# Selection masks built in one block behind the search, the l2 norm ahead of the tile copies, and an earlier first mixer load

## The chip, the core and the metric

The kernel runs on one core of a Trainium2 chip. Its engines work from queues of their own, in program order: PE (TensorE, matrix products into PSUM), ACT (ScalarE), DVE (VectorE), POOL (GpSimd), and SP (SyncE), which only issues DMAs here. They wait for each other by semaphores. The metric is device time of the program, in microseconds, as the median of the runs.

## The reference

Two layers of a streaming encoder run on 1,024 prompt tokens and on 8 x 16 sample tokens that carry caches and states, 1,152 tokens in all, 1,024 channels wide. A layer normalizes and modulates the tokens and makes one combined input projection. From it come three kinds of heads: gated DeltaNet (a delta rule in chunks of 64), softmax attention over selected keys, and an SSD mixer (Mamba-2, chunks of 64). Their outputs are joined by one output projection; a gated convolutional FFN follows.

What the change touches:

```
q, k = l2_normalize(silu(conv(q))), l2_normalize(silu(conv(k)))        # DeltaNet
score = sum_h relu(qi_h . ki) * wi_h          # indexer, per query and key
_, sel = top_k(score, 256)                    # ties go to the earlier key
att = softmax over the selected keys only
```

The kernel doesn't gather. For each block of 128 queries it finds the 256th largest score by a bitwise search, and builds a mask that is 0 at selected keys and -1e30 at all others; attention adds it to the logits.

## The kernel before

Channels lie on the partitions, tokens along the free dimension. One queue is written out by hand for each engine; all order below is program order.

**The dense tiles.** The input projection of a layer is 27 tiles of 128 output channels by 1,152 tokens, in `project` (L804), each from eight blocks of weights, into two PSUM sets in turn. Tile n+2 needs ACT's copy of tile n out of its set (`proj_evac`). Tiles 0 to 6 are rotated keys and queries; 7 and 22 to 26 are gates (`silu_tile`); 8 to 21 go through a causal convolution: ACT's `conv_rows` copies the tile into one of two `ext` buffers and makes the last tap, DVE's `conv` adds the other three, ACT's `conv_silu` finishes it.

**The l2 norm.** Five pieces i = 0 to 4 of q and k are squared by ACT (`l2_square`, in tile 9 + i), summed over each head by PE behind tile 10 + i (`l2_sums`, L927, into the same two PSUM banks each time), turned into 1/sqrt by ACT in tile 11 + i (`l2_scale`: Ln at L1550, Exp at L1552) and multiplied in by DVE (`l2_scaled`). `l2_sums(i)` waits for `l2_scale(i - 1)` (`l2_rs`). Piece 4 has 512 columns, the others 1,024.

**The search.** Seven score blocks (six of prompt queries with 384 to 1,024 keys, one of sample queries with 1,040; 5,264 columns together) are searched for the threshold `T`, 31 bits from the top. In a round DVE's `offer` makes a candidate and counts the first four blocks (L1880); ACT's `count_far` (L1560) counts the other three; DVE's `decide` waits for it and keeps or drops the bit. `ROUNDS` says how many rounds go with each tile from 8 on; DVE runs what is left after tile 21 without a break, ACT ahead of its gate tiles. `search_ties` ends the search. In tiles 16 to 18 PE also makes decay rows (`DEC_AT`), which DVE and ACT turn into decays; in 19 to 21 it makes key products (`KK_AT`), whose second pair waits for DVE's result of the first.

**After the tiles.** DVE zeroes `rt` (L2021, in the space of hT, so it waits for the last tile), multiplies the attention products by the decays (PE's L945 makes the products), then scales PE's natural copies of k (L982). POOL meanwhile inverts 32 x 32 blocks by elimination (L2371, L2373). SP loads the inverse into `rt` (L661) once it is zeroed. PE joins the blocks (L1003, L1009, then L1016), and the 16 DeltaNet chunks run.

**The masks.** `mask_piece(k, j)` is one of four pieces of the mask of block j: `mask_count` (a comparison with a count, L2048, a small instruction and an equality, L2051), `mask_scan` (running sum of equal scores, L2056), `mask_ties` and `mask_write` (L2068 last), seven instructions in all beside drains. Blocks 0 and 1 are done before the DeltaNet chunks; the pieces of blocks 2 to 6 are dealt out between the steps of the SSD mixer by `search()`: one behind the first state update of a tile and two behind its outputs. `t_cum` and `t_eq`, their working space, lie in hT.

**The SSD mixer.** Nine tiles of 128 tokens. For each PE makes decay rows and transposes (`ssd_rows`), ACT copies and exponentiates (`ssd_decay`), POOL scales (`ssd_scaled`, L2409, L2410) and carries the state (L2423), DVE adds the states, prepares (`ssd_prep`) and makes the outputs, ACT norms them (`ssd_norm`). SP's `load_s(t)` brings tile t into one of three slots `sl`, in turn; the first three are loaded once the DeltaNet output is done (`g_out`). The attention follows; PE waits for `mask_ready` ahead of its first logits.

Of the kernel before, what the change touches and what calls it, by code (L numbers as in the profile page):

```python
# [13 lines left out]
TOK = TPR + NB * TS  # L14
# [5 lines left out]
TOPK = 256  # L20
# [9 lines left out]
BIG = 1.0e30  # L30
# [2 lines left out]
NU, NUP = 36, 32  # L33
GW = 24
G_G, G_DT, G_BETA = 0, 12, 20
ROUNDS = {8: 2, 9: 2, 10: 2, 11: 2, 12: 2, 13: 2, 14: 2, 15: 2, 16: 1, 17: 1, 18: 1, 19: 1, 20: 1, 21: 1, 22: 3, 23: 3, 24: 3}
FAR = (4, 5, 6)
SHARED = sum(ROUNDS.values())
DEC_AT = {16: (0, 1), 17: (2, 3), 18: (4, 5)}
# [120 lines left out]
def build(nc, a):  # L160
# [3 lines left out]
    with ctx:  # L164
# [59 lines left out]
        one_t = sb("one_t", [128, 1])  # L224
# [195 lines left out]
        def turned(d, i):  # L420
            return ptb[d % 2][:, 512 * i:512 * i + 512]

        t_cum = hw[:, 0:1040]
        t_eq = hw[:, 1040:2080]
        far_signs = {j: xw[:, o:o + SC_N[j] // 2].bitcast(bf16) for j, o in ((4, 7952), (5, 7432), (6, 7432))}


# [39 lines left out]

            return ap.rearrange("p h (c t) -> p h c t", t=64)

        sl = [z.rearrange("p (c k x) -> p c k x", c=2, k=12) for z in (xw[:, 7432:8968], hw[:, 4840:6376], big[:, 2 * TOK:2 * TOK + 1536])]  # L470

        def two_tiles(x, c, k):

# [13 lines left out]
        hs_scaled = [big[:, o_qk + 1024 * q:o_qk + 1024 * q + 1024] for q in range(3)] + [fext[:, 0:1024]]  # L487
        def tile_in(t):

            return sl[(t + 1) % 3], sl_in[(t + 1) % 3], t // 3 + 1  # L490

        hb = [xw[:, 4096 + 512 * i:4608 + 512 * i] for i in range(3)]
        h_end = xw[:, 5632:6144]
# [64 lines left out]
        def _(sp):  # L558
# [28 lines left out]
            for l in range(NL):  # L587
# [92 lines left out]
                sp.wait_ge(*g_wtc.at(l, 5))  # L680
                for hp in range(2):
                    sp.dma_start(gt[:, hp, :], a["scr"][14 + hp]).then_inc(*gt_in.up())
                sp.wait_ge(*g_out.at(l, 3))
                for t in range(3):
                    load_s(t)
                sp.dma_start(hs, a["sstate"][l]).then_inc(*state_in.up())
                for t in range(3, NT):
# [703 lines left out]
        def _(sc):  # L1391
# [61 lines left out]
            for l in range(NL):  # L1453
# [91 lines left out]
                def l2_scale(i):  # L1545
                    m = TPR if i < 4 else 512
                    sc.wait_ge(*l2_sum.at(l, i + 1))
                    if i:
                        sc.wait_ge(*l2_mul.at(l, i))
                    act_(l2r[:, 0:m], PS[:, 3072:3072 + m], ACT.Ln, bias=eps_t[:, :])  # L1550
                    dr()
                    act_(l2r[:, 0:m], l2r[:, 0:m], ACT.Exp, scale=-0.5).then_inc(*l2_rs.up())  # L1552
# [10 lines left out]

                silu_tile(NROT)
                for n in range(LEAD, LEAD + NCONV):
                    conv_rows(n)
                    if 0 <= n - LEAD - 3 < 5:
                        l2_scale(n - LEAD - 3)
                    if n > LEAD:
                        conv_silu(n - 1)  # L1570
                        if n - LEAD - 1 < 5:
                            l2_square(n - LEAD - 1)
                    for k in DEC_AT.get(n, ()):
                        sc.wait_ge(*g_diff.at(l, k + 1))
                        x = dec_piece(k)
                        act_(x, x, ACT.Exp).then_inc(*g_dec.up())
                    for i in range(ROUNDS[n]):
                        count_far()
# [173 lines left out]
        def _(dv):  # L1752
# [57 lines left out]
            for l in range(NL):  # L1810
# [201 lines left out]
                for bit in bits:  # L2012
                    offer(bit)
                    decide(bit)
                search_ties()
                if l == 0:
                    dv.wait_ge(ada_kept.sem, 7)
                    add_bias(16, 28, mod)
# [22 lines left out]
                    dv.wait_ge(*g_eg.at(l, 3 * hp + 3))  # L2041
                    tt_(qkv[:, hp, :], qkv[:, hp, :], eg_row[:, hp, :], ALU.mult)
                dr().then_inc(*g_qe.up())
                def mask_count(j):
                    n = SC_N[j]
                    sco = scores[:, SC_OFF[j]:SC_OFF[j] + n]
                    thr = T[:, j:j + 1].bitcast(f32)
                    V.tensor_scalar(t_eq[:, 0:n], sco, thr, 0.0, ALU.is_gt, ALU.add, accum_out=CNT[:, j:j + 1])  # L2048
                    dr()
                    V.tensor_scalar(NEED[:, j:j + 1], CNT[:, j:j + 1], -1.0, float(TOPK), ALU.mult, ALU.add)  # L2050
                    V.tensor_scalar(t_eq[:, 0:n], sco, thr, None, ALU.is_equal)  # L2051
                    dr()

                def mask_scan(j):
                    n = SC_N[j]
                    V.tensor_tensor_scan(t_cum[:, 0:n], one_t[:, 0:1].to_broadcast([128, n]), t_eq[:, 0:n], 0.0, ALU.mult, ALU.add)  # L2056
                    dr()

                def mask_ties(j):
                    n = SC_N[j]  # L2060
                    stt(t_sel[:, 0:n], t_cum[:, 0:n], NEED[:, j:j + 1], t_eq[:, 0:n], ALU.is_le, ALU.mult)
                    dr()

                def mask_write(j):
                    n = SC_N[j]
                    stt(t_eq[:, 0:n], scores[:, SC_OFF[j]:SC_OFF[j] + n], T[:, j:j + 1].bitcast(f32), t_sel[:, 0:n], ALU.is_gt, ALU.add)
                    dr()
                    V.tensor_scalar(masks[:, SC_OFF[j]:SC_OFF[j] + n], t_eq[:, 0:n], -1.0, BIG, ALU.add, ALU.mult)  # L2068
                    dr()

                def mask_piece(k, j):
                    if k == 0:
                        mask_count(j)
                    elif k == 1:
                        mask_scan(j)
                    elif k == 2:
                        mask_ties(j)
                    else:
                        mask_write(j)

                for j in range(2):
                    for k in range(4):
                        mask_piece(k, j)

                V.memset(gS, 0.0)
                dr().then_inc(*g_s.up())
# [40 lines left out]
                    stt(mixT[:, 0:2, c0:c0 + m], o_n[:, :, c0:c0 + m], par[:, P_GNG:P_GNG + 1], gt[:, :, c0:c0 + m], ALU.mult, ALU.mult)  # L2127
                    dr().then_inc(*g_out.up())

                searched = []  # L2130

                def search():

                    k = len(searched)
                    j = 2 + k // 4
                    if j < 7:
                        searched.append(k)
                        mask_piece(k % 4, j)

                def ssd_prep(t):  # L2140

                    dv.wait_ge(*s["acted"].at(l, t + 1))
# [7 lines left out]
                for t in range(NT):  # L2150
                    if t < 8:
                        dv.wait_ge(*s["st"].at(l, t + 1))
                        for c in range(2):
                            n = 2 * t + c
                            dv.wait_ge(*s["he"].at(l, n + 1))
                            tt_(by_group(hb[(n + 1) % 3]), by_group(h_end), PS[:, 3072:4096].rearrange("p (g c x) -> p g c x", g=2, c=2)[:, :, c, :],
                                ALU.add).then_inc(*s["h"].up())
                            if c == 0:
                                search()
                        ssd_prep(t + 1)  # L2160
                    dv.wait_ge(*s["y"].at(l, t + 1))
                    need(dv, *s["nrm"].at(l, t))
                    tt_(eight(y1), eight(bank(5)), b3(gs[:, EGC, t, :], 64), ALU.mult)
                    dr()
                    tt_(y1, y1, bank(4), ALU.add)
                    dr()
                    tt_(y1, y1, bank(3), ALU.mult)
                    dr().then_inc(*s["y2"].up())
                    search()
                    search()  # L2170
                dv.wait_ge(*s["he"].at(l, 17))
                for q in range(4):
                    dv.wait_ge(*s["hs"].at(l, q + 1))
# [2 lines left out]
                        PS[:, 3072:4096].rearrange("p (g b x) -> p b g x", g=2, b=2)  # L2176
                    tt_(two, hs_scaled[q].rearrange("p (b g x) -> p b g x", b=2, g=2), new, ALU.add).then_inc(*s["hsd"].up())

                while len(searched) < 4 * 5:
                    search()  # L2180
                dr().then_inc(*mask_ready.up())


                V.memset(qz, 0.0)
                dr()
                for h in range(4):
# [414 lines left out]
```

## Time and profile before

| | us |
|---|---|
| median of three runs | 4369.09 (4368.46 to 4374.56) |
| the profiled execution, its time | 4367.9 |
| its span in the profile | 4365.8 |
| mean granted clock of TensorE in it | 0.961 |

The span is what the profiler saw between the first and the last instruction; the execution's own time has 2.1 us around it. Times in the rows below are microseconds from the start of the span. The first layer's dense tiles 7 to 26 run from about 296 to 667, its SSD mixer from about 755 to 880; the second layer repeats this some 2,150 us later.

### The profile page before, as it was taken

The numbers are of one execution on the slowest core, as the hardware profiler recorded it, in microseconds if no ns is written. First come the engines' busy times: TensorE is split into PE (matmuls) and PEld (weight loads), VectorE is DVE, ScalarE is ACT, GpSimd is POOL, SyncE is SP. The second block draws the span as 40 slices with busy tenths as digits, with TensorE's granted clock in tenths as the row PEclk, the third lists the DMA queues.
The fourth block names the chain that finished last, engine by engine and source line by source line (L and its number), as shares of the span: only waits on it lengthen the run. The fifth ranks groups of instructions, "written<-read, shape, count | busy, mean of one in ns | idle before, by whom it ended". The sixth has DMA issues, their size and how long they took to land.

```text
span 4365.8 us, 49384 instructions
## 1 busy us (share of the span) xinstructions
PE 4051.1 (93%) x20340; PEld 2189.5 (50%) x20340; DVE 1397.9 (32%) x2792; ACT 979.6 (22%) x1659; POOL 260.9 (6%) x384
## 2 busy tenths in 40 slices
PE   6788898889999999999999979978899999999998
PEld 3454456645455555555545435565454555554554
DVE  2236674662311111100022456647513212121001
ACT  2026662431100000000011366434301000000000
POOL 0000031400000000000000000414000000000000
PEclk9899998899999999999999989978999999999999
DMA  5410133142122122111122101423311111111111
GB/s 200 114 60 29 36 96 99 59 175 102 60 97 87 59 68 68 59 51 42 57 74 76 59 25 56 123 74 113 117 41 41 34 34 34 34 34 32 36 36 52
DMA packets 186849, 299.48 MB, mean 69 GB/s; under 512 B 89056, under 2 KB 140448, under 8 KB 180224
## 3 DMA queue, kind: packets, MB, share of 16 engines
q1 hardware_dynamic: 182144, 279.35, 19.5%
q0 software_dynamic: 3904, 12.27, 0.9%
q10 hardware_dynamic: 576, 4.72, 0.3%
q8 instruction: 160, 2.62, 0.3%
q14 instruction: 65, 0.53, 0.0%
HBM read 245.30 MB, written 42.47 MB: 66 GB/s over the span
## 4 chain that ended last, share of the span: by engine, by line
PE 87%; DVE 4%; ACT 2%; issue 2%; POOL 1%; DMA 1%; DVEq 1%; ACTq 1%; SPq 1%; POOLq 0%
PE PS L804 51%; PE PS L1380 16%; PE PS L1351 6%; PE PS L832 2%; PE PS L782 1%; PE PS L1227 1%; DVE big L1768 1%; PE PS L927 1%; DVE xT L1771 1%; PE PS L1281 1%; PE PS L1305 1%; POOL xT L2423 1%; DVE hT L1771 1%; PE PS L1264 1%; PE PS L1246 1%
## 5 line engine op out<-in xcount | busy, mean ns | idle before, releaser
L804 PE MATMUL PS<-hT,ring 128*128 128x512 f32 (+1 forms) x6816 | 2243.7, 491 | 34.6 <-ACT hT L1449 21.2
L804 PEld LDWEIGHTS PS<-hT,ring 128*128 128x128 f32 x6816 | 1135.3, 192 | 1152.1 <-issue 1138.0
L1380 PE MATMUL PS<-big,ring 128*128 128x512 f32 (+1 forms) x2112 | 683.5, 487 | 2.5 <-DVE big L1771 2.5
L1380 PEld LDWEIGHTS PS<-big,ring 128*128 128x128 f32 x2112 | 346.6, 191 | 339.4 <-issue 336.5
L1768 DVE SCALAR_TENSOR_TENSOR xT<-PS,mod,xT 128x1024 f32<-128x1024 f32 x32 | 41.1, 1284 | 856.9 <-PE PS L1380 642.0
L1437 ACT ACTIVATE hT<-xT 128x1152 f32<-128x1152 f32 x40 | 46.3, 1162 | 929.0 <-DVEq L2288 804.2
L1351 PE MATMUL PS<-big,ring 128*128 128x512 f32 (+1 forms) x768 | 250.3, 487 | 1.0 <-DVEq L2227 1.0
L2316 DVE TENSOR_SCALAR big<-fext,par 128x1024 f32<-128x1024 f32 x44 | 35.7, 812 | 671.2 <-ACTq L1736 671.2
L1560 ACT ACTIVATE xT<-big,tk 128x1024 bf16<-128x1024 f32 x186 | 223.5, 1202 | 52.0 <-DVEq L1908 47.2
L1734 ACT ACTIVATE fext<-PS 128x1024 f32<-128x1024 f32 x44 | 45.1, 1025 | 839.8 <-PE PS L804 839.8
L1880 DVE TENSOR_SCALAR_CACHE_REDUCE xT<-big,tk 128x384 bf16<-128x384 f32 (+6 forms) x268 | 222.8, 832 | 28.0 <-issue 0.9
L1771 DVE TENSOR_TENSOR big<-big,PS 128x1152 f32<-128x1152 f32 x44 | 59.6, 1354 | 442.0 <-PE PS L804 442.0
L1351 PEld LDWEIGHTS PS<-big,ring 128*128 128x128 f32 x768 | 126.7, 191 | 124.7 <-issue 123.2
L2454 POOL DMA_DIRECT2D out_o_ftail<-ftail x44 | 23.8, 540 | 1918.3 <-DVEq L2326 1918.3
L1768 DVE SCALAR_TENSOR_TENSOR big<-fext,par,big 128x1024 f32<-128x1024 f32 (+1 forms) x176 | 136.1, 815 | 6.8
L1740 ACT ACTIVATE big<-big 128x1152 f32<-128x1152 f32 x44 | 51.2, 1163 | 193.6 <-DVEq L2322 193.6
L927 PE MATMUL PS<-big,cf 128*128 128x512 f32 x36 | 30.4, 986 | 60.1 <-ACT big L1552 60.1
L782 PE MATMUL PS<-ring,silc 128*32 128x128 f32 x1536 | 63.4, 301 | 23.9 <-DMA ring<-in_w_ada 22.7
L1768 DVE SCALAR_TENSOR_TENSOR big<-big,par 128x1024 f32<-128x1024 f32 x96 | 74.3, 816 | 33.7 <-ACTq L1529 30.7
L1771 DVE TENSOR_TENSOR xT<-xT,PS 128x512 f32<-128x512 f32 (+2 forms) x108 | 58.7, 548 | 65.1 <-PE PS L1177 23.9
L1768 DVE SCALAR_TENSOR_TENSOR xT<-big,par,xT 128x1024 f32<-128x1024 f32 x72 | 55.7, 814 | 65.5 <-ACTq L1529 63.4
L832 PE MATMUL PS<-big,hT 128*128 128x276 f32 x288 | 67.8, 395 | 0.3 <-ACT mod L1417 0.3
(384 smaller groups left out, 3253.4 us busy)
## 6 DMA issues: line engine op xcount, KB each, us to landing
ring<-in_w_ada SPq DMA_DIRECT2D x96, 512.0 KB, 4.9
ring<-in_w_in SPq DMA_DIRECT2D x54, 512.0 KB, 5.2
ring<-in_w_gate SPq DMA_DIRECT2D x44, 512.0 KB, 3.5
ring<-in_w_up SPq DMA_DIRECT2D x44, 512.0 KB, 3.5
ring<-in_w_down SPq DMA_DIRECT2D x32, 448.0 KB, 3.3
d_x<-big SPq DMA_DIRECT2D x24, 576.0 KB, 4.6
ring<-in_kidx SPq DMA_DIRECT2D x16, 512.0 KB, 4.8
ring<-in_w_out SPq DMA_DIRECT2D x16, 512.0 KB, 5.6
```

The source lines that it names most:

```text
L782: i = mm(PS[32 * m:32 * m + 32, where:where + 128], silc[:, 2 * q + k, :], w[:, m, k, :], start=(q == 0 and k == 0), stop=(q == 3 and k == 1))
L804: i = mm(pset(n % 2)[:, c0:c0 + m], w[:, k, :], hT[:, k, c0:c0 + m], start=(k == 0), stop=(k == KT - 1))
L832: i = mm(bank(7 - t % 2, VW), hT[:, k, t * 128:(t + 1) * 128], wv[:, k, :], start=(k == 0), stop=(k == KT - 1))
L927: x = mm(PS[:, 3072 + c0:3584 + c0], b64, l2s[i % 2][:, c0:c0 + 512], start=True, stop=True)
L1351: i = mm(pset(m % 2)[:, c0:c0 + n], w[:, k, :], mixT[:, k, c0:c0 + n], start=(k == 0), stop=(k == KT - 1))
L1380: i = mm(pset(m % 2)[:, c0:c0 + n], w[:, k - k0, :], act[:, k * TOK + c0:k * TOK + c0 + n], start=(k == 0), stop=(k == NF - 1))
L1437: act_(sqb[k % 2], xT[:, k, :], ACT.Square).then_inc(*sq_ready.up())
L1560: act_(far_signs[j], scores[:, SC_OFF[j]:SC_OFF[j] + SC_N[j]], ACT.Sign, scale=SCALE[:, j:j + 1], bias=BIAS[:, j:j + 1], accum_out=CNT[:, ...
L1740: act_(aj, aj, ACT.Silu).then_inc(*ff_silu.up())
L1768: return V.scalar_tensor_tensor(out=out, in0=in0, scalar=scalar, in1=in1, op0=op0, op1=op1)
L1771: return V.tensor_tensor(out, in0, in1, op)
L1880: V.tensor_scalar(t_sel[:, 0:SC_N[j]], scores[:, SC_OFF[j]:SC_OFF[j] + SC_N[j]], limit[:, j:j + 1].bitcast(f32), 0.0, op, ALU.add, accum_o ...
```

## The change

All seven masks are built in one block on DVE right behind `search_ties`, and `mask_ready` is signalled there; the pieces are gone from before the DeltaNet chunks and from the SSD steps, with `search()` itself. Since hT is still read by the last dense tiles at that point, `t_cum` and `t_eq` move to the two `ext` buffers. `ROUNDS` gives tiles 16, 18 and 20 a second round, and tile 24 loses its three: six rounds in place of nine are left after tile 21. On ACT, `l2_scale` comes ahead of `conv_rows` in the same tile. On SP, `load_s(0)` goes ahead of the wait for `g_out`, and the slots change places so that tile 0 lies in free space.

```diff
-ROUNDS = {8: 2, 9: 2, 10: 2, 11: 2, 12: 2, 13: 2, 14: 2, 15: 2, 16: 1, 17: 1, 18: 1, 19: 1, 20: 1, 21: 1, 22: 3, 23: 3, 24: 3}
+ROUNDS = {8: 2, 9: 2, 10: 2, 11: 2, 12: 2, 13: 2, 14: 2, 15: 2, 16: 2, 17: 1, 18: 2, 19: 1, 20: 2, 21: 1, 22: 3, 23: 3}
...
-        t_cum = hw[:, 0:1040]
-        t_eq = hw[:, 1040:2080]
+        t_cum, t_eq = [ext[p][:, 0:1040] for p in range(2)]
...
-        sl = [z.rearrange("p (c k x) -> p c k x", c=2, k=12) for z in (xw[:, 7432:8968], hw[:, 4840:6376], big[:, 2 * TOK:2 * TOK + 1536])]
+        sl = [z.rearrange("p (c k x) -> p c k x", c=2, k=12) for z in (xw[:, 7432:8968], big[:, 2 * TOK:2 * TOK + 1536], hw[:, 4840:6376])]
...
-            return sl[(t + 1) % 3], sl_in[(t + 1) % 3], t // 3 + 1
+            return sl[t % 3], sl_in[t % 3], t // 3 + 1
...
                     sp.dma_start(gt[:, hp, :], a["scr"][14 + hp]).then_inc(*gt_in.up())
+                load_s(0)
                 sp.wait_ge(*g_out.at(l, 3))
-                for t in range(3):
+                for t in range(1, 3):
                     load_s(t)
...
                 for n in range(LEAD, LEAD + NCONV):
-                    conv_rows(n)
                     if 0 <= n - LEAD - 3 < 5:
                         l2_scale(n - LEAD - 3)
+                    conv_rows(n)
                     if n > LEAD:
...
                 search_ties()
+
+                def mask_count(j):
...
+                for j in range(7):
+                    mask_count(j)
+                    mask_scan(j)
+                    mask_ties(j)
+                    mask_write(j)
+                dr().then_inc(*mask_ready.up())
                 if l == 0:
                     dv.wait_ge(ada_kept.sem, 7)
                     add_bias(16, 28, mod)
...
-                for j in range(2):
-                    for k in range(4):
-                        mask_piece(k, j)
...
                                 ALU.add).then_inc(*s["h"].up())
-                            if c == 0:
-                                search()
...
                     dr().then_inc(*s["y2"].up())
-                    search()
-                    search()
...
-                while len(searched) < 4 * 5:
-                    search()
-                dr().then_inc(*mask_ready.up())
+                dr()
```

The four functions `mask_count` to `mask_write` are moved unchanged.

## Rows read from the trace of the kernel before

**Rows 1.** The page: span, and costliest groups (busy us, mean ns, idle before, releaser).
```profile
span 4365.8 us, 49384 instructions
...
L927 PE MATMUL PS<-big,cf 128*128 128x512 f32 x36 | 30.4, 986 | 60.1 <-ACT big L1552 60.1
```
**Rows 2.** Windows around PE's head sums: length, busy time per engine, granted clock.
```profile
360.80:362.80 2.00, 2.00 (x8) 1.04 (x7) 1.77 (x5) 1.70 (x3) 0.00 (x0) 1.00 0.36 92
...
385.77:389.52 3.75, 3.75 (x5) 1.68 (x6) 1.44 (x3) 3.65 (x4) 0.00 (x0) 0.50 0.00 0
```
**Rows 3.** Timeline of ACT, tiles 11 and 12: start, length, instruction, [idle before <-releaser].
```profile
374.32 0.19 ACT L1560 ACTIVATION_READ_ACCUMULATOR xT<-big,tk 128x1 f32 x1
...
380.81 1.28 ACT L1550 ACT_TABLE_LOAD   x1
...
385.64 1.28 ACT L1533 ACT_TABLE_LOAD   x1
...
405.41 1.02 ACT L1523 ACTIVATE big<-PS 128x1024 f32<-128x1024 f32 x1 [7.15 <-PE PS L804]
...
424.85 0.18 ACT L1560 ACTIVATION_READ_ACCUMULATOR xT<-big,tk 128x1 f32 x1
```
**Rows 4.** Timeline of DVE, tile 15 to the zeroing of rt.
```profile
500.12 3.43 DVE L1771 TENSOR_TENSOR tk<-tk 128x7 f32<-128x7 f32 x1
...
524.00 0.17 DVE L1771 TENSOR_TENSOR tk<-tk 128x7 int32<-128x7 f32 x1 [4.48 <-ACTq L1562]
...
555.31 0.17 DVE L1771 TENSOR_TENSOR tk<-tk 128x7 int32<-128x7 f32 x1 [4.48 <-ACTq L1562]
...
591.27 4.79 DVE L1768 SCALAR_TENSOR_TENSOR big<-big,par 128x1024 f32<-128x1024 f32 x6 [3.73 <-ACTq L1529]
...
597.65 0.17 DVE L1771 TENSOR_TENSOR tk<-tk 128x7 int32<-128x7 f32 x1
...
602.55 0.17 DVE L1771 TENSOR_TENSOR tk<-tk 128x7 int32<-128x7 f32 x1 [0.30 <-ACTq L1562]
...
645.36 0.21 DVE L1771 TENSOR_TENSOR tk<-tk 128x7 int32<-128x7 f32 x1 [0.30 <-ACTq L1562]
...
667.75 1.98 DVE L2021 MEMSET hT<- 128x2304 f32 x1 [15.55 <-PE PS L804]
```
**Rows 5.** Timeline of DVE, the masks of blocks 0 and 1.
```profile
688.58 0.61 DVE L2048 TENSOR_SCALAR_CACHE_REDUCE hT<-big,tk 128x384 f32<-128x384 f32 x1
...
692.73 0.75 DVE L2048 TENSOR_SCALAR_CACHE_REDUCE hT<-big,tk 128x512 f32<-128x512 f32 x1
...
693.63 0.48 DVE L2051 TENSOR_SCALAR hT<-big,tk 128x512 f32<-128x512 f32 x1
...
704.30 0.29 DVE L1771 TENSOR_TENSOR big<-PS,gq 128x128 f32<-128x128 f32 x1 [6.44 <-PE PS L1042]
```
**Rows 6.** Timeline of PE: attention products, first join, first SSD tile.
```profile
668.44 4.42 PE L945 MATMUL PS<-xT 64*64 64x64 f32 x144 [1.24 <-ACTq L1514]
...
687.19 2.21 PE L1003 MATMUL PS<-xT,hT 32*32 32x32 f32 x128 [0.69 <-ACT hT L1597]
...
759.49 0.48 PE L1118 MATMUL PS<-hT 128*64 128x64 f32 x4 [0.78 <-DMA hT<-d_x]
```
**Rows 7.** Timeline of SP: the first loads into rt.
```profile
673.71 2.69 SPq L661 DMA_DIRECT2D hT<-d_r  x4
```
**Rows 8.** Windows of the SSD steps: all eight tiles, two single steps.
```profile
778.07:872.99 94.92, 80.92 (x988) 57.18 (x988) 65.54 (x81) 45.19 (x166) 46.71 (x43) 0.84 0.17 54
...
789.36:801.90 12.54, 12.54 (x123) 8.76 (x123) 8.43 (x13) 4.82 (x18) 5.07 (x5) 0.59 0.03 11
...
852.13:862.48 10.35, 8.73 (x126) 6.14 (x125) 6.04 (x9) 6.46 (x24) 5.98 (x7) 1.00 0.01 2
```
**Rows 9.** Timelines in layer 0: a DVE mask instruction beside POOL; a POOL elimination.
```profile
824.11 2.32 DVE L2051 TENSOR_SCALAR hT<-big,tk 128x1024 f32<-128x1024 f32 x1
...
633.23 0.70 POOL L2373 TENSOR_TENSOR big<-big,xT 128x255 f32<-128x255 f32 x1
```

More of the change, by code:

```diff
@@ L2015, in _, with mask_scan, mask_ties, mask_write @@
                 search_ties()
+                def mask_count(j):
+                    n = SC_N[j]
+                    sco = scores[:, SC_OFF[j]:SC_OFF[j] + n]
+                    thr = T[:, j:j + 1].bitcast(f32)
+                    V.tensor_scalar(t_eq[:, 0:n], sco, thr, 0.0, ALU.is_gt, ALU.add, accum_out=CNT[:, j:j + 1])
+                    dr()
+                    V.tensor_scalar(NEED[:, j:j + 1], CNT[:, j:j + 1], -1.0, float(TOPK), ALU.mult, ALU.add)
+                    V.tensor_scalar(t_eq[:, 0:n], sco, thr, None, ALU.is_equal)
+                    dr()
+                def mask_scan(j):
+                    n = SC_N[j]
+                    V.tensor_tensor_scan(t_cum[:, 0:n], one_t[:, 0:1].to_broadcast([128, n]), t_eq[:, 0:n], 0.0, ALU.mult, ALU.add)
+                    dr()
+                def mask_ties(j):
+                    n = SC_N[j]
+                    stt(t_sel[:, 0:n], t_cum[:, 0:n], NEED[:, j:j + 1], t_eq[:, 0:n], ALU.is_le, ALU.mult)
+                    dr()
+                def mask_write(j):
+                    n = SC_N[j]
+                    stt(t_eq[:, 0:n], scores[:, SC_OFF[j]:SC_OFF[j] + n], T[:, j:j + 1].bitcast(f32), t_sel[:, 0:n], ALU.is_gt, ALU.add)
+                    dr()
+                    V.tensor_scalar(masks[:, SC_OFF[j]:SC_OFF[j] + n], t_eq[:, 0:n], -1.0, BIG, ALU.add, ALU.mult)
+                    dr()
+                for j in range(7):
[4 more added lines that the diff above has]
+                dr().then_inc(*mask_ready.up())
                 if l == 0:
@@ L2043, in _ @@
                 dr().then_inc(*g_qe.up())
[L2044 to L2079, printed above, removed]
-                for j in range(2):
-                    for k in range(4):
-                        mask_piece(k, j)
                 V.memset(gS, 0.0)
@@ L2128, in _ @@
                     dr().then_inc(*g_out.up())
[L2130 to L2138, printed above, removed]
                 def ssd_prep(t):
@@ L2177, in _ @@
                     tt_(two, hs_scaled[q].rearrange("p (b g x) -> p b g x", b=2, g=2), new, ALU.add).then_inc(*s["hsd"].up())
-                while len(searched) < 4 * 5:
-                    search()
-                dr().then_inc(*mask_ready.up())
+                dr()
                 V.memset(qz, 0.0)
```

## The prediction

> **What bounds the kernel now.** The page first: PE is busy nearly all the span, but its line for the head sums (L927, `l2_sums`) is small in work and large in idle time before it: 60.1 us behind ACT's L1552, the last instruction of `l2_scale` [rows 1]. The code says where: four sums in each of two layers, so 7.5 us apiece, after dense tiles 11 to 14. In the windows the reader sees what the wait does to PE: the first set of sums runs in 2.0 us at a granted clock of 1.00 (2.4 GHz), the next, behind 7.5 us of idling, in 3.75 us at 0.50 (1.2 GHz) [rows 2].
>
> ACT's timeline explains the wait [rows 3]. ACT counts for the search until 374.5, then idles until tile 11 is out of PE; it copies that tile, and only then (380.81) begins the two table loads, Ln and Exp of the norm, done at 385.64. PE stands through copy and norm. At tile 12 ACT idled 7.15 us before the copy, time in which the 4.83 us norm would have fitted.
>
> DVE's timeline gives the search [rows 4]: one decision every 15.65 us in tiles 16 to 18, then nine rounds of 5.3 us on average, an end at 652.2 and 15.55 us of idling until PE has left hT. Then come the masks of blocks 0 and 1 [rows 5], the joins [rows 6], and the SSD steps, where the other five masks are cut into pieces [rows 8].
>
> **The norm ahead of the copies.** Nothing is added; PE no longer waits for copy plus norm. ACT then becomes the limit: its whole chain for a tile, from the copy at 405.41 to the end of the second count at 425.03, is 19.6 us with norm, copies, Silu, square and both counts [rows 3], in any order. Today some 7.5 us of idling come on top, 27.1 a tile; of these PE works 15.9 on the tile itself (27.1 less 7.5 of wait and 3.75 of sums [rows 2]) and, kept busy, 2.0 on the sums. So a tile takes 19.6 us in place of 27.1, with PE idling under 2 us in each. What is queued behind the norm on ACT is the copy of the tile just made; the norm's own input has been there since the tile before, so it doesn't hold the copy. PE's gain is some 30 us a layer at tile 15. It is worth that only if the search and everything behind it on ACT and DVE keeps up, so I follow this chain to the point where PE needs DVE again.
>
> **Search and masks.** From 374.5: tiles 11 to 14 at 19.6 give 452.9; tile 15 (half the norm, no square) about 17.5: 470.4. There DVE was held 3.4 us in a seven-element instruction [rows 4], right where the code lets POOL begin its decay products (L2387, after `l2_mul`); the same can be expected: 473.8. Tiles 16 to 18 at 15.65, and a second round in 16 and in 18 at 4.9 each (the step from 597.65 to 602.55): 530.6. Tiles 19 to 21 took 42.3 together (555.31 to 597.65), of which 3.7 was a wait for PE that is gone when DVE is late, and 20 gets a second round: 574.1. In the trace this is 597.65: DVE's chain keeps 23.5 of the 30 us. Six rounds are left in place of nine, at 5.3 (nine took 47.7): 605.9. From the last decision to the search's end is 6.8: 612.7.
>
> Mask 0 takes 4.15 us for 384 columns; mask 1 and a zeroing of 0.2 end 6.44 us before 704.30, which leaves it 4.95 for 512 [rows 5]: 0.8 more for each 128. Over the 5,264 columns of all seven that makes 45.2 us. The ext buffers that now hold sums and equalities change no instruction's size. POOL eliminates blocks under the first four masks (its elimination starts when tile 21's products are done, and shifts with them); in a mask made beside POOL one comparison of 1,024 columns took 2.32 us, where 512 columns took 0.48 alone, and POOL's own instructions are at most 0.70 there [rows 5, 9]. Below, contention costs nothing; above, five of a mask's seven instructions each wait out one such instruction, 14 us over four masks. I take 3, because the search's small instructions beside POOL lengthened a round from 4.9 to only 5.3 on average. So the masks end at 661.
>
> PE would be through its tiles near 640 (30 us off, less some 3 for which tile 20's products wait for the later DVE). It finds DVE in the masks: behind them are queued the zeroing of rt, the attention products (on which PE's natural copies wait) and thereby SP's block loads. So PE stands some 20 us: most of what the norm freed is given back here. What counts is the zeroing: 661 in place of 667.75.
>
> From the zeroing to the first join, PE's L1003, it is 19.4 us now [rows 4, 6]. PE has the 4.4 us of L945 [rows 6] behind it by then, as well as part of the natural copies: at best 15.0. But it has idled, and rows 2 show half clock after 7.5 us of that: at worst 20, all as slow as it gets back. I take 17.3. SP's first block load went out at 673.71 [rows 7], and all had landed by 687.19, within 13.5 us; now the first can go at about 663, so they are in by 676.5. The join is then at 678.3 in place of 687.2: 8.9 us a layer.
>
> **Masks gone from the mixer steps.** Blocks 0 and 1 begin at 688.58, under PE's joins, which start at 687.19, and behind them DVE waits 6.44 us for PE [rows 5, 6]: removing them gives nothing there. In the SSD steps eight tiles take 94.9 us [rows 8]. The two windows show the kinds of step: 10.35 us at clock 1.00, where the loop is the y products, ACT's norm and decay, POOL's scaling, DVE's state; and 12.54 us at 0.59, where PE is busy throughout. Without pieces of masks, DVE is never late. All steps of the first kind: 82.8, a gain of 12.1; alternating kinds: 91.6, a gain of 3.3. In the first kind PE idles only 1.6 us, so I take 8.
>
> **The early mixer load.** One issue on SP moves ahead of a wait; SP's later loads are not delayed by it, and the other two slots change places at equal sizes. PE's wait for this load is 0.78 us [rows 6]: 0.8 gained, because PE first makes its decay rows, which hid the rest of the transfer. Masks ready earlier serve nobody: PE and SP ask for them after the SSD outputs. The moved bias addition (0.3 us in layer 0) is read much later.
>
> **Sum.** 8.9 + 0.8 + 8 = 17.7 us a layer; the second layer shows the same wait, so 35.4. The profiled execution took 4367.9 (span 4365.8), 1.2 below the median of 4369.09, a difference smaller than what counts here: 4332. About 0.2% (9 us) is what a measurement of this kernel tells from no change.
>
> Bounds: masks from 654.8 (no POOL hold, no contention) with a join 15.0 later and SSD 12.1 give 30.3 a layer, 4307. Masks at 675.8 (all 14 us, and a second hold of 3.4) with 20 and 3.3 lose 4.5 a layer, 4377.
>
> **Rivals.** *Masks held by POOL:* contention is the full 14 us, the masks end at 672, the join at 689.3, 2.1 us later than now; 8.8 stays from the other two, 6.7 a layer: 4354. For it speaks the 2.32 us comparison; against it the search's rounds. 0.18.
> The Trainium skill, SBUF — State Buffer, section Who interferes with whom, says that a VectorE instruction with two SBUF inputs, or in a two-port mode, shuts out a GpSimd instruction that reads SBUF, and the reverse, for its whole length. By that rule the five contending instructions of each mask would wait, and this rival's time would hold; the 2.32 us row agrees with a whole-length block, while the mean lengthening of a round doesn't tell.
>
> *More comes through:* no hold, no contention, PE quick after its wait, SSD all at the short step: 4307 as in the bound. Against it: the hold is in the trace, and the code's order keeps it. 0.17.
>
> *No change:* the time is only moved to the zeroing of rt. That takes masks ending 17.7 us later, near 679: 4368. Seven masks would have to take 66 us. 0.07.
>
> *Slower:* ACT's queue doesn't let the norm go early, since the second count waits for DVE's candidate, and the norm still ends 7.5 us behind PE's tile. Tiles 11 to 14 then keep 27.1 us, the masks end at 691, the join at 708.3, 21.1 us late: 12.3 lost a layer, 4392. It decides when each of these tiles saves under 3.1 of 7.5 us. Against it stand 7.15 us of idle ACT before the copy. 0.06.
>
> **How the numbers follow.** The forecast has 0.52, with a range of its own of 4320 to 4347 (masks 3 us either way, SSD 4). Outward to hold 8 in 10: 4308 takes in nearly the better case, 4356 the held masks. Faster: 0.52 + 0.18 + 0.17 = 0.87; same 0.07; slower 0.06.
>
> **What would show it.** L927 without idle time of more than 2 us and its sums under 2.1 us; the first tile copies 19 to 20 us apart in tiles 11 to 14; the search's end near 613 and the zeroing of rt near 661, straight behind the last mask, with no wait for PE; PE idle for 15 to 20 us behind tile 26; L1003 near 678; SSD steps of 10 to 11.5 us; no wait for the first SSD load. The prediction is wrong if DVE still idles before the zeroing, if the masks take over 55 us, or if the tile spacing stays above 22.

## The result, and the profile after

The change makes the kernel 0.9% faster: 4331.0 us, median of five runs (4326.9 to 4341.48), against 4369.09 for the kernel before; the ratio is 0.9915, with a 95% interval from 0.9899 to 0.9931. Forecast were 4332, in a range of 4308 to 4356. The profiled execution took 4328.62 us.

First two lines of the kernel before: the chain that ended last by engine, from its page, and the line of the head sums (least, median and greatest duration in ns, first and last start):

```profile
PE 87%; DVE 4%; ACT 2%; issue 2%; POOL 1%; DMA 1%; DVEq 1%; ACTq 1%; SPq 1%; POOLq 0%
```

```profile
L927 PE MATMUL PS<-big,cf x36: 592/1061/1193, 360.9 to 2618.8; 128*128 128x512 f32 x36
```

The same of the kernel after, with its span, and with PE's idle time before the head sums and the number of waits:

```profile
span 4326.8 us, 49376 instructions
...
PE 75%; DVE 10%; ACT 6%; issue 3%; DVEq 1%; ACTq 1%; POOL 1%; DMA 1%; SPq 0%; POOLq 0%
```

```profile
L927 PE MATMUL PS<-big,cf x36: 592/593/1061, 367.4 to 2574.3; 128*128 128x512 f32 x36
its engine sat idle before it (us, times) until:
  ACT big L1552: 11.1, 8
```

The 60.1 us in front of the head sums [rows 1] are down to 11.1, and the median of these products is down from 1061 ns to 593. But the chain that ends last now runs less over PE and more over the others: PE's share is down from 87% to 75%, DVE's is up from 4% to 10% and ACT's from 2% to 6%. In this execution all of the first layer runs some 6.5 us later than in the one before: the first head sums begin at 367.4 in place of 360.9, ahead of which the code is the same. Times of the first layer below stand as the trace gives them; the prediction's have 6.5 to be added.

ACT's timeline of the kernel after shows the norm's first table load (L1550) ahead of the copy of tile 11 (L1523), and the copies of tiles 12 to 14, each 19.9, 19.6 and 19.0 us behind the one before it. Its last three lines are the norm's first load in tile 15, the second count of tile 15 and the copy of tile 16:

```profile
381.06 1.28 ACT L1550 ACT_TABLE_LOAD   x1
...
385.78 1.01 ACT L1523 ACTIVATE big<-PS 128x1024 f32<-128x1024 f32 x1
...
405.72 1.00 ACT L1523 ACTIVATE big<-PS 128x1024 f32<-128x1024 f32 x1
...
425.31 1.01 ACT L1523 ACTIVATE big<-PS 128x1024 f32<-128x1024 f32 x1
...
444.27 1.00 ACT L1523 ACTIVATE big<-PS 128x1024 f32<-128x1024 f32 x1
...
458.33 1.28 ACT L1550 ACT_TABLE_LOAD   x1
...
475.22 1.24 ACT L1560 ACTIVATE xT<-big,tk 128x1024 bf16<-128x1024 f32 x1 [4.34 <-DVEq L1908]
...
479.25 1.02 ACT L1523 ACTIVATE big<-PS 128x1024 f32<-128x1024 f32 x1 [0.16 <-issue]
```

DVE's timeline of the kernel after: the instruction held in tile 15, the decision of tile 21 and the last decision of the search, the first mask instruction, a scan beside POOL, the zeroing of rt, and the first instruction of the DeltaNet chunks.

```profile
471.43 3.48 DVE L1905 TENSOR_SCALAR tk<-tk 128x7 int32<-128x7 int32 x1
...
580.33 0.17 DVE L1771 TENSOR_TENSOR tk<-tk 128x7 int32<-128x7 f32 x1
...
611.26 0.17 DVE L1771 TENSOR_TENSOR tk<-tk 128x7 int32<-128x7 f32 x1 [0.30 <-ACTq L1562]
...
618.72 0.61 DVE L2021 TENSOR_SCALAR_CACHE_REDUCE big<-big,tk 128x384 f32<-128x384 f32 x1
...
644.69 3.64 DVE L2029 TENSOR_TENSOR_SCAN big<-one_t,big 128x896 f32<-128x896 f32 x1
...
669.32 1.98 DVE L2055 MEMSET hT<- 128x2304 f32 x1 [0.59 <-issue]
...
702.86 0.29 DVE L1771 TENSOR_TENSOR big<-PS,gq 128x128 f32<-128x128 f32 x1 [16.05 <-PE PS L1042]
```

Where DVE idled 15.55 us for PE [rows 4], it now goes from the search into the masks and from these into the zeroing. The one that waits is PE, as its timeline behind tile 26 shows:

```profile
648.25 4.42 PE L945 MATMUL PS<-xT 64*64 64x64 f32 x144 [1.24 <-ACTq L1514]
652.50 2.97 PE L982 MATMUL PS<-cf,xT 64*64 64x64 f32 x96
672.13 7.57 PE L982 MATMUL PS<-cf,xT 64*64 64x64 f32 x192 [16.67 <-DVE hT L1771]
...
685.22 2.21 PE L1003 MATMUL PS<-xT,hT 32*32 32x32 f32 x128 [0.69 <-ACT hT L1597]
```

PE is through its tiles 20 us sooner than before on the clock (648.25 against 668.44 [rows 6]), stands 16.67 us, and joins only 2.0 sooner (8.4 with the later start taken off). The windows of the SSD steps (length; busy time and count of PE, weight loads, DVE, ACT and POOL; granted clock, DMA share, GB/s), the same stretch as in [rows 8] and a single step:

```profile
775.12:858.38 83.26, 70.03 (x988) 50.33 (x988) 30.35 (x46) 45.19 (x166) 39.98 (x43) 0.98 0.18 62
785.48:795.84 10.36, 8.83 (x128) 6.25 (x127) 4.04 (x6) 5.96 (x22) 4.13 (x5) 1.00 0.23 77
```

Eight steps take 83.3 us in place of 94.9, all of them of the short kind.

To compare the kernels, distances between first instructions free the stages from the start. "Join" is from the first head sum (L927) to the first join (L1003); "SSD" is from the first products of the SSD mixer (L1118) to the first outputs of its last tile (L1192). First and second layer are given apart; the differences are to the kernel before on the same chip (median). The kernels in the lower rows are those of the experiments.

| kernel | us | to the kernel before | join | SSD |
|---|---|---|---|---|
| before | 4369.09 | | 326.3 / 327.3 | 109.8 / 109.7 |
| after | 4331.0 | -38.1 | 317.9 / 314.9 | 97.1 / 98.6 |
| norm alone | 4305.73 | -67.1 | 295.5 / 294.6 | 109.8 / 105.0 |
| norm late | 4402.34 | +29.5 | 351.9 / 351.0 | 97.0 / 96.8 |
| spread | 4315.82 | -57.0 | 298.3 / 297.4 | 109.4 / 109.5 |
| spread, outputs | 4291.98 | -80.9 | 296.8 / 299.6 | 97.0 / 97.0 |
| spread, gaps | 4290.37 | -82.5 | 296.0 / 294.2 | 96.9 / 98.9 |
| no elimination | 4317.75 | -55.1 | 311.3 / 309.6 | 99.1 / 98.6 |

From the first head sums to the output projection (first L1351) the layers went from 656.5 and 658.6 us to 635.7 and 634.4: 20.8 and 24.2 gained.

### The profile page after: what moved, and what is told of

Same layout as the page of the kernel before. It is cut to its first block, busy times and chain, and to the rows that moved or that the text cites. A ratio compares the mean times of both kernels' runs of the same rounds, so it can differ in the third digit from the quotient of the medians.

```text
span 4326.8 us, 49376 instructions
## 1 busy us (share of the span) xinstructions
PE 4025.7 (93%) x20330; PEld 2178.6 (50%) x20340; DVE 1394.8 (32%) x2792; ACT 978.3 (23%) x1659; POOL 279.3 (6%) x384
## 3 DMA queue, kind: packets, MB, share of 16 engines
q1 hardware_dynamic: 182144, 279.35, 19.6%
## 4 chain that ended last, share of the span: by engine, by line
PE 75%; DVE 10%; ACT 6%; issue 3%; DVEq 1%; ACTq 1%; POOL 1%; DMA 1%; SPq 0%; POOLq 0%
PE PS L804 40%; PE PS L1380 16%; PE PS L1351 6%; ACT xT L1560 3%; DVE big L1768 2%; PE PS L832 2%; DVE xT L1880 1%; PE PS L782 1%; PE PS L1227 1%; DVE big L1771 1%; POOL xT L2401 1%; PE PS L1281 1%; PE PS L1305 1%; DVE xT L1771 1%; DVE big L2029 1%
## 5 line engine op out<-in xcount | busy, mean ns | idle before, releaser
L1351 PE MATMUL PS<-big,ring 128*128 128x512 f32 (+1 forms) x768 | 250.3, 487 | 1.0 <-DVEq L2205 1.0
L1351 PEld LDWEIGHTS PS<-big,ring 128*128 128x128 f32 x768 | 126.7, 191 | 124.7 <-issue 123.2
L782 PE MATMUL PS<-ring,silc 128*32 128x128 f32 x1536 | 62.5, 298 | 24.7 <-DMA ring<-in_w_ada 24.2
L1469 ACT ACTIVATE big<-PS 128x1152 f32<-128x1152 f32 x14 | 15.8, 1130 | 216.5 <-PE PS L804 115.5
```

What stands on the lines that cost most here:

```text
L782: i = mm(PS[32 * m:32 * m + 32, where:where + 128], silc[:, 2 * q + k, :], w[:, m, k, :], start=(q == 0 and k == 0), stop=(q == 3 and k == 1))
L1351: i = mm(pset(m % 2)[:, c0:c0 + n], w[:, k, :], mixT[:, k, c0:c0 + n], start=(k == 0), stop=(k == KT - 1))
```

## The experiments

**The norm alone, and everything but the norm.** The first kernel is the one before with only the norm moved; the second is the change with the norm back behind the copies.

```diff
 # norm alone (on the kernel before); norm late is the reverse (on the kernel after)
                 for n in range(LEAD, LEAD + NCONV):
-                    conv_rows(n)
                     if 0 <= n - LEAD - 3 < 5:
                         l2_scale(n - LEAD - 3)
+                    conv_rows(n)
```

> The kernel before with the norm ahead of the tile copies and nothing else. My theory, that the later of PE's tiles and DVE's chain sets the zeroing of rt: the search ends within 5 us of where it does with the whole change (as many rounds, in another order), some 25 us before PE is through its tiles; DVE waits there for PE, the zeroing of rt comes near 645, and the join 19.4 behind it. That is 27 to 30 us a layer, with the SSD steps as before: 4309 to 4315. Rival, that the norm in itself brings only what the whole change gained up to the join (8.5 and 12.5 us in the two layers): 4348. Rival, that only the idle time in front of the head sums comes back (49 us in all): 4320.

> The whole change, but the norm behind the copies as before: the masks' block, the rounds and the early load without the norm. My theory: tiles 11 to 14 take 27.1 us again, the search ends near 648 to 655, the masks take 49.6 behind it, PE stands some 30 us behind tile 26, and the join comes 25 to 30 us later than before; the SSD gives 13 back and the attention loses 1.4. Some 15 us a layer are lost: 4390 to 4408. Rival, that the block is hidden by DVE's 15.6 us of idling and by PE's tiles: only the SSD gain shows, 4345.

Measured: 4305.73 for the norm alone, ratio 0.9849 (0.9834 to 0.9864), and 4402.34 for the rest without it, ratio 1.0059 (1.0043 to 1.0076). DVE and PE of the norm alone:

```profile
642.71 1.98 DVE L2021 MEMSET hT<- 128x2304 f32 x1 [15.35 <-PE PS L804]
```

```profile
643.41 4.42 PE L945 MATMUL PS<-xT 64*64 64x64 f32 x144 [1.24 <-ACTq L1514]
...
662.99 2.21 PE L1003 MATMUL PS<-xT,hT 32*32 32x32 f32 x128 [0.70 <-ACT hT L1597]
```

One moved call on ACT is worth more than the whole change: the join comes 31 and 33 us sooner. DVE waits for PE, and PE no longer for DVE. The theory holds, and its two rivals fall. The gain, 67.1 us, is above the 54 to 60 expected, since the join came sooner than the 27 to 30 us a layer that I had; in the second layer the SSD mixer is also 4.8 us shorter than in the first with the same code, and why stays open. One part of the theory was wrong: the search ended at 627.1, 8.3 us later behind the first head sums than with the whole change, where I had said within 5; that leads to the last experiment. PE of the norm late:

```profile
710.83 7.46 PE L982 MATMUL PS<-cf,xT 64*64 64x64 f32 x192 [17.03 <-DVE hT L1771]
```

The masks' block then ends at 707 and the join comes 25.6 and 23.7 us later than before, while the SSD gains its 12.8 all the same. The time is as expected, but PE's wait is 17.03 us and not some 30. The block behind the search is a loss that the norm pays for.

**The masks where DVE idles.** Blocks 0 to 3 stay behind the search, block 4 goes ahead of the DeltaNet chunks, 5 and 6 into the SSD steps in pieces, one a step behind the first state update. This version and the two that follow keep the early load and deal the rounds out as the kernel before does; behind the block the working space is back in hT, and `mask_ready` is signalled behind the SSD mixer. The cuts below leave these lines out.

```diff
-                for j in range(7):
+                for j in range(4):
                     mask_count(j)
...
+                for piece in pieces:
+                    piece(4)
                 V.memset(gS, 0.0)
...
                             dv.wait_ge(*s["he"].at(l, n + 1))
                             tt_(...).then_inc(*s["h"].up())
+                            if c == 0:
+                                pieces[t % 4](5 + t // 4)
```

> The norm early and the masks spread over the places where DVE idles: blocks 0 to 3 behind the search, block 4 ahead of the DeltaNet chunks (16.05 us of idling there), the pieces of blocks 5 and 6 one per SSD step behind its first state update (3.6 us of idling there); rounds as before, the early load kept. My theory: the block behind the search ends near 643, PE's tiles near 645, so PE no longer stands there; the join comes 17 us a layer earlier than with the whole change, and the SSD steps stay near 10.4 us: 4289 (4283 to 4300). Rival, that POOL's elimination or SP's loads hold the join near 680 anyway: 4320 or more. Rival, that pieces in the SSD steps cost there what they cost before: 4312.

Measured: 4315.82, ratio 0.9868 (0.9853 to 0.9883), near the last rival. The join came as expected; the SSD didn't gain anything (109.4), with one piece a step in place of three. POOL's timeline of a step shows why, with DVE's mask instructions of that step in the second fence. The third fence is a step of the next kernel, in which the pieces stand elsewhere (lines are one lower in these two kernels):

```profile
784.71 1.95 POOL L2391 TENSOR_TENSOR hT<-hT,gaf 128x512 f32<-128x512 f32 x1 [5.25 <-ACT hT L1634]
786.63 1.49 POOL L2392 TENSOR_TENSOR hT<-hT,gaf 128x512 f32<-128x512 f32 x1
788.29 1.04 POOL L2405 TENSOR_TENSOR xT<-xT,gaf 128x512 f32<-128x512 f32 x1 [0.18 <-issue]
```

```profile
784.48 1.28 DVE L1767 SCALAR_TENSOR_TENSOR hT<-big,tk,xT 128x1024 f32<-128x1024 f32 x1
785.84 1.37 DVE L2040 TENSOR_SCALAR big<-hT 128x1024 bf16<-128x1024 f32 x1
```

```profile
778.50 1.04 POOL L2391 TENSOR_TENSOR hT<-hT,gaf 128x512 f32<-128x512 f32 x1 [5.24 <-ACT hT L1634]
779.51 1.04 POOL L2392 TENSOR_TENSOR hT<-hT,gaf 128x512 f32<-128x512 f32 x1
780.73 1.04 POOL L2405 TENSOR_TENSOR xT<-xT,gaf 128x512 f32<-128x512 f32 x1 [0.18 <-issue]
```

DVE idles behind the first state update, but it does so because POOL scales there, and the step waits for POOL's L2405. The two instructions of a mask piece beside POOL's stretch two of these by 0.91 and 0.45 us, 1.4 us of this step; the eight steps together take 12.4 us more than with the pieces elsewhere.

**The same pieces behind the outputs, and no pieces between the steps.**

```diff
 # spread, outputs
-                            if c == 0:
-                                pieces[t % 4](5 + t // 4)
...
                     dr().then_inc(*s["y2"].up())
+                    if t < 8:
+                        pieces[t % 4](5 + t // 4)
 # spread, gaps: blocks 0 to 2 behind the search, 3 and 4 ahead of the chunks, and
+                for piece in pieces:
+                    piece(5)
                 ssd_prep(0)
...
                         ssd_prep(t + 1)
+                    else:
+                        for piece in pieces:
+                            piece(6)
```

> The spread masks once more, with one thing moved: the pieces of blocks 5 and 6 go from behind the first state update of an SSD step to behind the outputs of the tile, where DVE idles 2.35 us and POOL idles too. Theory 1, that a piece costs there nothing, and that behind the state update it cost by stretching POOL's scaling (1.04 to 1.95 us): the eight SSD steps come from 109.4 (first L1117 to first L1191) to 97 to 100, the join stays; 18 to 24 us less in all than with the pieces behind the state update, 75 to 81 under the kernel before. Rival, that any piece in a step costs its own length: no change, 57 under the kernel before.

> No pieces in the SSD steps at all: blocks 0 to 2 behind the search, 3 and 4 ahead of the DeltaNet chunks, 5 ahead of the first SSD preparation (8.5 us of idling), 6 in the last SSD tile ahead of its outputs (8.5 us of idling). Theory 1: PE waits for none of them; SSD 97 to 99, join 295 to 297 behind the first head sums; 78 to 84 under the kernel before, the best of all. Rival, that these gaps are too short with POOL at work beside them: 1 to 3 us lost at each of the three places, 65 to 75 under the kernel before.

Measured: 4291.98, ratio 0.9821 (0.9806 to 0.9836), and 4290.37, ratio 0.9817 (0.9803 to 0.9832). Both times lie where they were expected. The first version moves one thing and the SSD falls from 109.4 and 109.5 to 97.0 in both layers, about what it takes without any piece: the place of a piece was the whole cost, not its length. DVE's timeline of that kernel shows the last piece of a mask, two instructions, between the outputs and the state update; DVE is through 0.19 us before PE releases it:

```profile
785.61 1.28 DVE L1767 SCALAR_TENSOR_TENSOR hT<-big,tk,xT 128x1024 f32<-128x1024 f32 x1
786.97 0.69 DVE L2040 TENSOR_SCALAR big<-hT 128x1024 bf16<-128x1024 f32 x1
787.85 0.69 DVE L1770 TENSOR_TENSOR xT<-xT,PS 128x512 f32<-128x512 f32 x1 [0.19 <-PE PS L1176]
```

In the second, DVE has made three masks and zeroes rt all the same within 0.4 us of PE's first attention products (its own timeline, then PE's):

```profile
642.97 1.98 DVE L2056 MEMSET hT<- 128x2304 f32 x1 [0.59 <-issue]
```

```profile
642.64 4.41 PE L944 MATMUL PS<-xT 64*64 64x64 f32 x144 [1.24 <-ACTq L1513]
```

Both versions beat both kernels; between them the runs don't decide.

**POOL taken away from the masks.** POOL's elimination is left out.

```diff
-                eliminate(blk_b, blk_r, blk_x, 32, 1, range(31, 0, -1))
...
-                eliminate(sblk_b, sblk_r, sblk_x, 16, 2, range(15, 0, -1))
```

> The whole change with POOL's elimination left out (its subtractions are not made, so the inverted blocks stay the identity): nothing of POOL runs beside the masks but zeroing and a copy. My theory: the 49.6 us of the masks shrink to the 45.2 that the lone instructions add up to, the last six rounds from 5.15 to 4.9, and the join comes 5 to 6 us earlier in each layer: 4319 to 4322. Rival, that the masks are longer for another reason (the other buffers): 49.6 stays, 4331. Rival, that a whole-length block costs 14 us: more than 10 us a layer, under 4311.

Measured: 4317.75, ratio 0.9871 (0.9857 to 0.9886). DVE's first mask in it and its scan of 896 columns, and in the next two fences, from the kernel after, the equality and scan of the first mask with POOL beside them and POOL's copy beside the scan of 896 (3.64 us above):

```profile
613.55 0.61 DVE L2021 TENSOR_SCALAR_CACHE_REDUCE big<-big,tk 128x384 f32<-128x384 f32 x1
...
614.31 0.41 DVE L2024 TENSOR_SCALAR big<-big,tk 128x384 f32<-128x384 f32 x1
614.80 0.96 DVE L2029 TENSOR_TENSOR_SCAN big<-one_t,big 128x384 f32<-128x384 f32 x1
...
636.92 2.02 DVE L2029 TENSOR_TENSOR_SCAN big<-one_t,big 128x896 f32<-128x896 f32 x1
```

```profile
619.48 0.70 DVE L2024 TENSOR_SCALAR big<-big,tk 128x384 f32<-128x384 f32 x1
620.26 1.35 DVE L2029 TENSOR_TENSOR_SCAN big<-one_t,big 128x384 f32<-128x384 f32 x1
```

```profile
644.04 2.40 POOL L2373 COPY big<-big 128x1024 f32<-128x1024 f32 x1
```

The masks take 45.3 us (613.5 to 658.8) in place of 49.6 (618.7 to 668.3), and the join comes 6.6 and 5.3 us sooner. The last six rounds take 5.03 us on average instead of 5.15 (4.9 expected). This bears the theory out, and rules out that the buffers lengthen the masks. The time is 55 us under the kernel before, that of the whole change by 38; of the 17 between them the joins account for 12, and the other 5 stay open. POOL's copy of 2.40 us is in this kernel too, but it is done before the first mask.

**The early load undone.**

```diff
-                load_s(0)
                 sp.wait_ge(*g_out.at(l, 3))
-                for t in range(1, 3):
+                for t in range(3):
                     load_s(t)
```

> The whole change with the first mixer load behind its old wait. My theory: PE's first SSD products wait some 0.8 us for the load, 1 to 2 us in all, which only the trace can tell. Rival, that the load is hidden anyway: no wait. Rival, that the wait is longer now, as the steps in front of it came together: 3 us or more a layer.

One run: 4331.97. PE's first products of the SSD mixer in the two layers (lines one lower):

```profile
755.74 0.48 PE L1117 MATMUL PS<-xT 128*64 128x64 f32 x4 [0.68 <-DMA xT<-d_x]
```

```profile
2888.70 0.48 PE L1117 MATMUL PS<-xT 128*64 128x64 f32 x4 [1.23 <-DMA xT<-d_x]
```

The kernel after has no such wait; 1.9 us in all, as expected, and less than the times can show.

**The order of the rounds.** The whole change with the rounds dealt out as before, then four corners on one chip: masks in the block or in the gaps, rounds as changed or as before.

```diff
-ROUNDS = {..., 16: 2, 17: 1, 18: 2, 19: 1, 20: 2, 21: 1, 22: 3, 23: 3}
+ROUNDS = {..., 16: 1, 17: 1, 18: 1, 19: 1, 20: 1, 21: 1, 22: 3, 23: 3, 24: 3}
```

> The whole change with the rounds dealt out as before (one in tiles 16, 18 and 20, nine behind tile 21). By the step of my prediction the order makes 1.2 us of difference: within 3 us of the whole change, 38 to 43 under the kernel before. Rival, from the run with the norm alone, where the search ended at 627.1 in place of 618.7: the masks' block ends 8 us later, so does the join, and the whole is 16 us slower, 24 to 28 under the kernel before.

Measured: 4340.85, ratio 0.9926 (0.9908 to 0.9943), between the two expectations. The trace speaks for the rival: the masks begin 8.6 us later behind the first head sums, and the joins come at 324.2 and 323.7. DVE, ahead of PE once more, waits for tile 20 (2.53 us) and for tile 21, shown here, and the rounds that are not done in these waits stand behind them:

```profile
568.27 4.80 DVE L1768 SCALAR_TENSOR_TENSOR big<-big,par 128x1024 f32<-128x1024 f32 x6 [4.33 <-ACTq L1529]
```

> The whole change once more, as one corner of four on one chip: masks in one block behind the search or in the gaps, rounds as changed or as before. Where masks are in the block, DVE's chain sets the join, so an earlier end of the search counts in full. Expected 36 to 42 under the kernel before.

> Masks in one block, rounds as before. If the order of the rounds counts, as the first pair of traces says (search 8 us, join 6 to 9 us later in each layer): 10 to 16 slower than the corner with the changed rounds. If it doesn't, as I had it: within 3.

> Masks in the gaps, rounds as before. PE's tiles set the join, with 10 us to spare for DVE between the search and the zeroing only if block 2 is not counted: expected 78 to 84 under the kernel before, as in the run with this arrangement.

> Masks in the gaps, rounds as changed. Theory: with PE setting the join the earlier search brings nothing, and what it costs PE shows (waits for the key products that DVE then makes later, 2 to 5 us a layer): 4 to 10 slower than the corner with the old rounds. Rival, that the earlier search also shortens this version: 4 or more faster.

| masks, rounds | us | ratio (95%) | join |
|---|---|---|---|
| block, as changed | 4331.62 | 0.9911 (0.9897 to 0.9924) | 318.0 / 314.7 |
| block, as before | 4344.31 | 0.9938 (0.9924 to 0.9951) | 324.2 / 323.2 |
| gaps, as before | 4294.27 | 0.9819 (0.9805 to 0.9832) | 294.7 / 294.3 |
| gaps, as changed | 4298.05 | 0.9832 (0.9819 to 0.9846) | 300.6 / 297.6 |

With the block the changed order brings 12.7 us, as the rival had it; my 1.2 is refuted. With the gaps it seems to cost: the medians are 3.8 us apart, but their intervals overlap; the joins of the two profiles come 5.9 and 3.3 us later. Part of that is PE's wait for the key products, which DVE then makes later:

```profile
550.87 1.15 PE L944 MATMUL PS<-xT 64*64 64x64 f32 x32 [3.01 <-DVEq L2005]
```

So the same rounds help where DVE sets the join, and don't help, or hurt, where PE does. The times expected of the third and the fourth corner were missed by a little (77.1 under the kernel before, not 78 to 84, and 3.8 slower than the third, not 4 to 10).

## Why the prediction was right, point by point

- **The norm.** Tiles at 19.9, 19.6, 19.0 and 17.9 us (forecast 19.6, then 17.5 for tile 15), ACT idle only for the 1.0 to 1.4 us ahead of its second count that were in the 19.6 too. Waits in front of the sums reached 2.5 us where 2 was the bound, and one set of sums took 3.33 at the lower clock.
- **The chain to the search's end.** The hold (3.48 us) came in the tile where it was put, and with 6.5 added the forecast has tile 21's decision at 580.6 and the search's end at 619.2, the trace 580.33 and 618.72. The parts are right too: tile 15 with its hold took ACT 20.9 us (458.33 to 479.25), the 17.5 and 3.4 that I gave it. It ended 1.1 us sooner than forecast (480.3), as tiles 11 to 14 took 77.3 in place of 78.4, and from there to tile 21's decision it took 101.1 where I had 100.3. The worth of the rounds' order is inside this chain; the 1.2 us that I gave it in an expectation left out that DVE, ahead again, waits for PE (2.53 and 4.33 us in tiles 20 and 21).
- **The masks.** 45.2 plus 3 for contention; measured 49.6, and 45.3 with POOL away: the sum of lone instructions was right, contention 1.4 too small. The two bounds of the masks' end are 654.5 and 675.3 by the prediction's own terms, not 654.8 and 675.8, which moves its times by 1 us at most.
- **PE's stand and the join.** 16.67 us of 15 to 20; from the zeroing to the join 15.9 against 17.3. The join's gain was 8.4 in the first layer (forecast 8.9) and 12.4 in the second. The second has no bias addition behind the masks, its search ends 2.0 us sooner behind the head sums, and in the kernel before its join came 1.0 later than the first layer's.
- **Masks 0 and 1 ahead of the chunks.** Worth nothing, as said: DVE now idles 16.05 us there, and the chunks begin no sooner behind the join.
- **The SSD steps.** The mis-sized term: "Without pieces of masks, DVE is never late" had the range 3.3 to 12.1, of which I took 8. Measured are 12.7 and 11.1 by the distances above, since all steps are of the short kind. PE busy throughout in every other step was no bound of its own: those steps came from the pieces behind the state update.
- **The early load.** 0.8 forecast, 0.68 and 1.23 shown.
- **Not foreseen.** The attention takes 1.4 and 1.2 us longer than before (first L1227 to first L1351); over the kernels of the experiments, whose attention is the same, this stretch varies from 134.0 to 141.1 us, so that no cause can be read from one trace; it stays open.
- **The sum.** 17.7 a layer were forecast, 20.8 and 24.2 came, so 45.0 in place of 35.4. The total was nonetheless hit because this execution started its first layer 6.5 us late; that the time came within a few us is luck, as far as these two profiles tell. Over fourteen profiles the first head sums begin between 360.9 and 371.9, the kernel before being the earliest and the third corner next with 362.2; whether the changed kernels start later as a rule can't be told from the one profile of the kernel before.
- **The rivals.** Masks held by POOL: direction right, price not. Fourteen us were to be lost in four masks; 2.6 were, and 1.6 in the fifth. The Trainium skill, SBUF — State Buffer, section Who interferes with whom, exempts a VectorE instruction with at most one SBUF input outside the two-port modes. The Trainium skill there counts tensor_scalar among those that can enter such a mode, but not the form that writes out an accumulator. Of two that contend, the Trainium skill says, the one that comes second waits until the first is through. The trace agrees in kind: beside POOL the count, which has an accumulator, stays at 0.61 us, the equality goes from 0.41 to 0.70, the scan from 0.96 to 1.35. I had charged every one of five instructions a whole POOL instruction of 0.70, 3.5 us a mask; the first mask lost 1.3 and the fourth under 0.1. The largest wait came from POOL's one copy of 2.40 us (the scan of 896 at 3.64 instead of 2.02). *More comes through* was right in the SSD steps and nearly right in PE's way from the zeroing to the join (15.9, its best was 15.0), but the hold and the contention came. *No change* asked for masks of 66 us, *slower* for tiles of 27.1.

## What to carry to other kernels

Move the work that holds the busy engine first and alone, and look where the slack then lies: here one moved call was worth 67 us, and what was packaged with it, the masks' block above all, took 29 away again. Idle time of an engine is only room for other work if the engine it waits for isn't disturbed by that work: behind the state update DVE idled 3.6 us because POOL was on the path, and one piece a step there cost as much as three pieces a step had, while behind the outputs it was free. An order that helps while one engine sets the end may hurt when another does, so it has to be tried again after each step.

## What the runs showed of the hardware that was not expected

- The harm between DVE and POOL goes both ways, and counts by who is on the path: the elimination, at most 0.70 us an instruction when alone, lengthened the first four masks by 2.6 us and the copy behind it the fifth by 1.6, while one mask instruction made POOL's scaling 1.95 us instead of 1.04, and the SSD step waited for it.
- The granted clock can differ between two executions of the same code. These windows, of the kernel before and then of the one after, lie ahead of all that the change touches, about from the first products of L875 to those of L908:

```profile
265.00:290.00 25.00, 20.37 (x197) 11.50 (x195) 3.71 (x9) 5.67 (x6) 0.00 (x0) 1.00 0.48 169
```

```profile
267.00:295.00 28.00, 23.08 (x194) 11.96 (x192) 3.76 (x9) 5.78 (x6) 0.00 (x0) 0.87 0.42 151
```

PE makes nearly as many products, in 20.37 us at 1.00 and in 23.08 at 0.87. Of the 6.5 us by which the kernel after comes late to its first head sums, some 3 arise here. Why the clock differs stays open; a difference of some us between two profiles ahead of a change need not be an effect of the change.
